# A projection of un-normed activations: moving the RMS factor behind the expert query product

## What is computed

```python
h = x + mixed                                   # mixed: output projection of the attention block
return h + peer_ffn(rmsnorm(h, norm2_gain), peer_w_q, peer_sub_keys, peer_u, peer_v)

def _rms(x):
    return xf * lax.rsqrt(jnp.mean(xf * xf, axis=-1, keepdims=True) + EPS)
def rmsnorm(x, gain):
    return _rms(x) * gain

def peer_ffn(x, w_q, sub_keys, expert_u, expert_v):
    q = _rms((xt @ w_q).reshape(T, P_HEADS, P_KEY_DIM))     # 8 heads of 256
    s1 = einsum('thd,hnd->thn', q[..., :half], sub_keys[:, 0])
    s2 = einsum('thd,hnd->thn', q[..., half:], sub_keys[:, 1])
    ...                                         # top 16 of each half, then of their sums, softmax
    a = einsum('cd,ckd->ck', xc, expert_u[ec])  # the normed x again
    return einsum('ck,ckd->cd', g * gelu(a), expert_v[ec])
```

## Time and profile before

| | |
|---|---|
| median of 3 runs | 2245.87 us |
| lowest and highest run | 2237.79 and 2246.01 us |
| span of the profiled execution | 2240.8 us |
| PE busy in it | 2181.3 us, 97% |
| DVE busy | 1581.9 us, 71% |
| ACT busy | 1063.3 us, 47% |
| POOL busy | 501.9 us, 22% |

### The profile page before, as it was taken

The page is one execution under the profiler, slowest core; times in us unless marked ns, Lnnn a source line. Parts: engine busy times, 40 slices in busy tenths (PEclk is TensorE's granted clock), DMA queues, the critical chain, the costliest instruction groups (busy, mean ns, idle before and its releaser), DMA issues.

```text
span 2240.8 us, 35063 instructions
## 1 busy us (share of the span) xinstructions
PE 2181.3 (97%) x12495; PEld 1938.3 (87%) x12495; DVE 1581.9 (71%) x3249; ACT 1063.3 (47%) x1934; POOL 501.9 (22%) x387
## 2 busy tenths in 40 slices
PE   6999999999999988899999999999999999999999
PEld 4888888888878446668899999999999999999999
DVE  5444444433366687452488899999988899999996
ACT  5444344323243477633444445888864333333332
POOL 0000000000030000010000123655435555555550
PEclk9999999999999999999999999999999999999999
DMA  5222222222234100023355888999999999999993
GB/s 177 90 94 93 84 84 85 93 94 94 94 129 160 57 1 1 1 63 116 109 178 163 256 259 303 371 401 386 397 340 404 414 399 389 397 395 389 396 401 139
DMA packets 134241, 475.74 MB, mean 212 GB/s; under 512 B 14448, under 2 KB 30832, under 8 KB 132192
## 3 DMA queue, kind: packets, MB, share of 16 engines
q1 hardware_dynamic: 74592, 232.29, 30.1%
q0 software_dynamic: 55920, 212.36, 24.8%
q10 hardware_dynamic: 3600, 29.36, 3.2%
HBM read 422.58 MB, written 50.86 MB: 211 GB/s over the span
## 4 chain that ended last, share of the span: by engine, by line
PE 90%; DVE 7%; ACT 2%; issue 1%; DMA 0%; ACTq 0%; DVEq 0%
PE bank L469 18%; PE bank L471 17%; PE bank L470 17%; PE bank L1190 8%; PE bank L1192 8%; PE bank L1191 8%; PE bank L1162 4%; PE bank L484 2%; PE bank L584 1%; DVE wlo L456 1%; PE bank L544 1%; DVE rows L2207 1%; PE bank L778 1%; PE bank L796 1%; ACT pair_prob L1416 1%; PE bank L761 1%
## 5 line engine op out<-in xcount | busy, mean ns | idle before, releaser
L469 PE MATMUL bank<-act_hi,whi 128*128 128x352 f32 (+1 forms) x1968 | 713.9, 363 | 9.9 <-DVE act_lo L1688 5.8
L470 PE MATMUL bank<-act_lo,whi 128*128 128x352 f32 (+1 forms) x1968 | 702.6, 357 | 0.0
L471 PE MATMUL bank<-act_hi,wlo 128*128 128x352 f32 (+1 forms) x1968 | 702.4, 357 | 0.0
L456 DVE TENSOR_TENSOR wlo<-raw,whi 128x1024 fp32r<-128x1024 f32 x398 | 485.2, 1225 | 269.3 <-ACT whi L452 267.3
L452 ACT ACTIVATE whi<-raw 128x1024 fp32r<-128x1024 f32 x398 | 418.7, 1057 | 394.5 <-PE bank L1192 330.9
L469 PEld LDWEIGHTS bank<-act_hi,whi 128*128 128x128 f32 x1968 | 370.5, 188 | 59.2 <-issue 18.2
L471 PEld LDWEIGHTS bank<-act_hi,wlo 128*128 128x128 f32 x1968 | 370.2, 188 | 37.7
L470 PEld LDWEIGHTS bank<-act_lo,whi 128*128 128x128 f32 x1968 | 370.7, 188 | 35.9 <-issue 0.5
L1190 PE MATMUL bank<-h_hi,whi 128*128 128x384 f32 x1024 | 342.5, 334 | 1.8 <-issue 1.8
L1191 PE MATMUL bank<-h_lo,whi 128*128 128x384 f32 x1024 | 342.5, 334 | 0.0
L1192 PE MATMUL bank<-h_hi,wlo 128*128 128x384 f32 x1024 | 342.5, 334 | 0.0
(11 more groups left out here) (377 smaller groups left out, 2522.0 us busy)
## 6 DMA issues: line engine op xcount, KB each, us to landing
raw<-tiles SPq DMA_DIRECT2D x398, 512.0 KB, 4.9
gates_dram<-stage ACTq DMA_DIRECT2D x12, 2048.0 KB, 11.8
wg<-gates_dram POOLq DMA_DIRECT2D x16, 1536.0 KB, 13.3
acts_dram<-gelu SPq DMA_DIRECT2D x120, 192.0 KB, 5.7
hf<-acts_dram POOLq DMA_DIRECT2D x30, 768.0 KB, 10.4
bias<-alibi POOLq DMA_DIRECT2D x16, 256.0 KB, 2.9
w1s<-cmp_w POOLq DMA_DIRECT2D x1, 4096.0 KB, 13.3
res<-x_t ACTq DMA_DIRECT2D x4, 512.0 KB, 6.1
```

Source lines behind the costliest of these rows:

```text
L456: dve.tensor_tensor(wlo[:, j.slot, :], raw[:, j.slot, :], whi[:, j.slot, :].bitcast(F32), ALU.subtract).then_inc(lo_made, 1)
L469: pe.matmul(to, wh, x, start=(kc == 0), stop=False)
L470: pe.matmul(to, wh, xl, start=False, stop=False)
L471: last = pe.matmul(to, wl, x, start=False, stop=(kc == KC - 1))
```

## The change

The query projection takes `res * gain` instead of the normed input.

- As each J_E result is added to the residual, ACT also writes `raw_hi` = res * gain rounded, and DVE `raw_lo`, the rest (`make_raw_lo`). All 16 jobs of J_F multiply these. The two first jobs are no longer interleaved.
- POOL adds up the squares of all eight chunks (chunks 1 to 7 onto chunk 0, now in `sqe`), and PE sums them with one `add_squares` between jobs 0 and 1 of J_F. Four narrow matmuls beside it put the same sums in token order in bank 7, from which DVE makes EPS * (mean + EPS) as `eps_col`.
- The root, the Newton step and the normed input `xnrm` (two buffers, one chunk for each job) are made beside jobs 0 to 8 of J_F; `turn_x` stands inside jobs 2 to 9. J_U waits for all eight low parts.
- The head norm's `ms` adds `eps_col` in place of EPS.
- `raw_lo` lies where `subk` goes, so POOL loads `subk` when job 15 of J_F is done, in place of job 1.

```diff
@@ pool
-            for c in range(1, 6):
-                add_up(sq, 3 * KC + c + 1, c)
+            for c in range(1, KC):
+                add_up(sqe, 3 * KC + c + 1, c)
 
-            pool.wait_ge(job_done, J_F + 1 + RING)
+            pool.wait_ge(job_done, J_F + 16 + RING)
             pool.dma_start(subk[:, :, :], sub_keys).then_inc(S("subk_landed"), 16)
@@ tensor
-            for m, chunk in enumerate((0, 6, 7)):
-                pe.wait_ge(*((S("sq_added"), 15) if m == 0 else (sq_made, 3 * KC + chunk + 1)))
-                last = add_squares(4, sq[:, chunk, :], m == 0, m == 2)
-            last.then_inc(sums_made, 1)
+            def width_sums():
+
+                pe.wait_ge(S("sq_added"), 10 + KC - 1)
+                for tt in range(TT):
+                    pe.matmul(bank[7][:, 2 * tt:2 * tt + 2], sqe[:, 0, tt * P:(tt + 1) * P], ones[:, 0:2],
+                              start=True, stop=True)
+                add_squares(4, sqe[:, 0, :], True, True).then_inc(sums_made, 1)
...
-            two_jobs(Job(J_F), Job(J_F + 1), 3 * KC, turn_x)
+            multiply(pe, Job(J_F), raw_hi, raw_lo, chunk_normed(3 * KC))
+            width_sums()
+            multiply(pe, Job(J_F + 1), raw_hi, raw_lo)
             for m in range(2, 16):
-                multiply(pe, Job(J_F + m), act_hi, act_lo)
+                beside = (lambda kc: turn_x(m - 2) if kc == 4 else None) if m - 2 < KC else None
+                multiply(pe, Job(J_F + m), raw_hi, raw_lo, beside)
+            pe.wait_ge(lo_act, 5 * KC)
@@ scalar
-                square(sq[:, m, :], res[:, m, :], sq_made)
-            root(6, 0, 4, D)
-            for c in range(8):
-                act.wait_ge(normed, 3 * KC + c + 1)
-                copy(act_hi[:, c, :], hg[:, c, :], hi_act)
+                square(sqe[:, m, :], res[:, m, :], sq_made)
+                copy(raw_hi[:, m, :], res[:, m, :], hi_act, g("norm2", m))
             for m in range(16):
                 j = Job(J_F + m)
                 make_hi(act, j.ahead())
+                if m == 0:
+                    root(6, 0, 4, D, xnrm[:, 0, :])
                 result_of(act, j)
...
+                if m < KC:
+                    act.wait_ge(normed, 3 * KC + m + 1)
+                    copy(act_hi[:, m, :], xnrm[:, m % 2, :], hi_act)
@@ vector
+            def make_raw_lo(kc):
+                dve.wait_ge(hi_act, 3 * KC + kc + 1)
+                dve.scalar_tensor_tensor(out=raw_lo[:, kc, :], in0=res[:, kc, :], scalar=g("norm2", kc),
+                                         in1=raw_hi[:, kc, :].bitcast(F32), op0=ALU.mult, op1=ALU.subtract)\
+                    .then_inc(lo_act, 1)
...
+                if m:
+                    make_raw_lo(m - 1)
+            make_raw_lo(7)
...
-            invert(6, 0)
-            split_activations(lambda kc: (res[:, kc, :], hg[:, kc, :]), "norm2", 0, 3 * KC)
             for m in range(16):
                 make_lo(dve, Job(J_F + m).ahead())
+                if m == 0:
+                    invert(6, 0, xnrm[:, 0, :], xnrm[:, 1, :])
+                    dve.tensor_scalar(eps_col, ..., EPS / D, EPS * EPS, ALU.mult, ALU.add)
+                if m < KC:
+                    if m >= 2:
+                        dve.wait_ge(S("x_step"), m - 1)
+                        dve.wait_ge(lo_act, 4 * KC + m - 1)
+                    dve.scalar_tensor_tensor(out=xnrm[:, m % 2, :], in0=res[:, m, :], scalar=g("norm2", m),
+                                             in1=rrow[:, 0, :], op0=ALU.mult, op1=ALU.mult).then_inc(normed, 1)
+                if 1 <= m <= KC:
+                    make_act_lo(xnrm[:, (m - 1) % 2, :], 4 * KC, m - 1)
```

More of the change, by code:

```diff
@@ L363, in two_layer_kernel @@
         subk = at("subk", R + 16 * KB, [P, 16, P])
+        raw_hi = at("raw_hi", R, [P, KC, T], F32R)
+        raw_lo = at("raw_lo", R + 16 * KB, [P, KC, T], F32R)
+        sqe = at("sqe", R + 64 * KB, [P, KC, T])
+        xnrm = at("xnrm", R + 96 * KB, [P, 2, T])
+        eps_col = mx[:, 0:TT]
         ssb = at("ssb", R, [P, 16, P])
@@ L697, in _ @@
             pool.dma_start(wukv[:, :, :, :], w_ukv).then_inc(S("w_mla_landed"), 16)
-            for c in range(1, 6):
-                add_up(sq, 3 * KC + c + 1, c)
-            pool.wait_ge(job_done, J_F + 1 + RING)
+            for c in range(1, KC):
+                add_up(sqe, 3 * KC + c + 1, c)
+            pool.wait_ge(job_done, J_F + 16 + RING)
             pool.dma_start(subk[:, :, :], sub_keys).then_inc(S("subk_landed"), 16)
-            power(2, 32)
+            power(3, 32)
             def load_gates(grp):
@@ L1100, in turn_x @@
                 cols_ = slice((kc % 4) * P, (kc % 4 + 1) * P)
-                turn(pe, bank[5 + kc // 4][:, cols_], hg[:, kc, 0:P], ident)
+                turn(pe, bank[5 + kc // 4][:, cols_], xnrm[:, kc % 2, 0:P], ident)
                 for s in range(4):
-                    x = pe.matmul(bank[(4, 7)[kc // 4]][32 * s:32 * s + EXTRA, cols_], hg[:, kc, P:FIRST], ident,
+                    x = pe.matmul(bank[(4, 7)[kc // 4]][32 * s:32 * s + EXTRA, cols_], xnrm[:, kc % 2, P:FIRST], ident,
                                   start=True, stop=True)
-                if kc == KC - 1:
-                    x.then_inc(S("x_step"), 1)
-            two_jobs(Job(J_F), Job(J_F + 1), 3 * KC, turn_x)
+                x.then_inc(S("x_step"), 1)
+            multiply(pe, Job(J_F), raw_hi, raw_lo, chunk_normed(3 * KC))
+            width_sums()
+            multiply(pe, Job(J_F + 1), raw_hi, raw_lo)
             for m in range(2, 16):
-                multiply(pe, Job(J_F + m), act_hi, act_lo)
+                beside = (lambda kc: turn_x(m - 2) if kc == 4 else None) if m - 2 < KC else None
+                multiply(pe, Job(J_F + m), raw_hi, raw_lo, beside)
+            pe.wait_ge(lo_act, 5 * KC)
             def u_job(n):
@@ L1115, in _ @@
             pe.wait_ge(S("halves_added"), 8)
-            pe.wait_ge(S("x_step"), 5)
+            pe.wait_ge(S("x_step"), KC + 4)
             for h in (0, 1, 2, 3, 4, 5, 6, 7):
@@ L1120, in _ @@
             u_job(1)
-            pe.wait_ge(S("x_step"), 7)
+            pe.wait_ge(S("x_step"), KC + 6)
             for b in range(2):
@@ L1135, in _ @@
             pe.wait_ge(S("subk_landed"), 16)
-            pe.wait_ge(ms_made, 2)
+            pe.wait_ge(ms_made, 3)
             routes(0)
@@ L1214, in _, with root @@
             make_hi(act, Job(0))
-            def root(n, slot, b, width):
+            def root(n, slot, b, width, mean=mean):
                 act.wait_ge(sums_made, n)
@@ L1529, in _ @@
                 act.sem_inc(acts_stored[slot], 16)
-            act.wait_ge(S("x_step"), 1)
+            act.wait_ge(S("x_step"), KC)
             for h in range(2):
@@ L2170, in _ @@
             dve.wait_ge(ssq_made, 4)
+            dve.wait_ge(ms_made, 1)
             for b in range(2):
                 sums = bank[(4, 7)[b]][:, :].rearrange("p (t j r) -> p t j r", t=TT, j=4)[:, :, :, 0:1]
-                dve.tensor_scalar(ms[:, 0:32].rearrange("p (t b j) -> p t b j", t=TT, b=2)[:, :, b, :],
-                                  sums.rearrange("p t j r -> p t (j r)"), 1.0 / 256, EPS, ALU.mult, ALU.add)\
+                dve.scalar_tensor_tensor(out=ms[:, 0:32].rearrange("p (t b j) -> p t b j", t=TT, b=2)[:, :, b, :],
+                                         in0=sums.rearrange("p t j r -> p t (j r)"), scalar=1.0 / 256,
+                                         in1=eps_col.unsqueeze(2).broadcast_to((P, TT, 4)), op0=ALU.mult, op1=ALU.add)\
                     .then_inc(ms_made, 1)
@@ L2213, in use_row @@
                                              op0=ALU.mult, op1=ALU.add).then_inc(S("row_used"), 1)
-            dve.wait_ge(S("x_step"), 5)
+            dve.wait_ge(S("x_step"), KC + 4)
             for tt in range(TT):
```

5 lines of the change are left out of this document (4 added, 1 removed).

## The result

The changed kernel takes 2220.85 us, the median of 12 runs (2217.93 to 2229.2). The kernel before, run between them on the same chip, takes 2237.06 us (12 runs, 2228.26 to 2247.23). The ratio is 0.9942, interval 0.9924 to 0.996.

The account below looks back on a forecast made before the run. PE, busy 97% of the span, was taken as the bound. Jobs 87.04, turns 5.56 and sums 1.73 us make 94.33 instead of 101.62, a gain of 7.3; 2245.87 - 7.3 = 2238.6 us, range 2229 to 2246.

Parts of the forecast that it names:

- The sum: PE from J_E's end to J_U's start: 101.62 us before, 94.33 us after, a gain of 7.3 us.
- sixteen jobs and eight `turn_x`: PE's work in J_F: 16 jobs at 5.44 us make 87.04 us, eight turns at 0.695 make 5.56 us.
- square sums: PE in J_F: one remaining sum 0.86 us plus four narrow matmuls 0.87, together 1.73 us, bounds 1.1 to 1.75.
- the narrow matmuls: Four two-column matmuls on PE, taken to count as eight 128 x 128 transposes: 0.87 us, lower bound 0.2.
- The clock: PE from J_E's end to J_U's start: granted clock 1.00 throughout, as 0.50 stood only behind PE's 3.7 us wait.
- The inputs: Start of J_F: PE never pauses; slack 1.7 us for chunk 7, 2.0 for POOL's sum; rival of a partial pause 12%.
- the rule of the Trainium skill: Two-input DVE and POOL SBUF instructions lock each other out; chunk 7's low part would come at 992.4, slack 0.5 us.
- my budget of 2.68 of 2.72 us: Jobs 0 to 3 of J_E: DVE's work of 0.69 + 1.23 + 0.76 us just fits the 2.72 us between jobs.
- `subk`: Load issued about 76 us later, landing after 5.1 us, cover 9 us before first `routes`; rival of late landing 3%.
- The gain reaches the end: Behind J_F all work hangs on PE, so a rigid shift: the 7.3 us also come off the span, to 2233.5 us.
- The level of the time: Whole kernel: 7.3 us off the median 2245.87 gives 2238.6 us, with spans and times spreading over some 8 us.
- Faster by over 0.5%: Whole kernel: faster by more than about 11 us needs a low draw of the runs on top of the gain; 15%.

Follow-up runs that it names:

- the second profile: The changed kernel run again without an edit: 2230.31 us, ratio 0.998 to the kernel before.
- `subk_late`: On the kernel before, only the `subk` load moved, to wait for job 15 of J_F in place of job 1: 2228.61 us, ratio 0.9994.
- `after`: First measurement and profile of the changed kernel, against the kernel before: 2220.85 us, ratio 0.9942; profiled span 2227.5 us.

## Why the prediction was wrong, point by point

**The sum: right.** Forecast 94.33 us from J_E's end to J_U's start; measured 94.38, and 94.39 in the second profile. Term by term: sixteen jobs and eight `turn_x` together 92.63 by the trace (94.38 less 1.75 of sums) against 92.60; square sums 1.75 against 1.73, the narrow matmuls 0.80 against 0.87. That they count as eight instructions was the upper bound that I took. In exchange the sum on PE took 0.95 us, forecast 0.86. The gain of this stretch is 7.24 us, forecast 7.3.

**The clock: right, and for the reason named.** 1.00 throughout. Both runs that bring a pause back show the granted clock below it again. I had seen it after a wait of 3.7 us; the runs show it after 2.8 as well.

**The inputs: no pause, as forecast, but a reading of the rows was wrong.** I took the 1.23 us of a weight split beside a 1.81 us addition on POOL as no slowing, and weighed against it the rule of the Trainium skill ("SBUF — State Buffer", section "SBUF: two separate sides"), which these rows seemed to refute. I had looked at DVE's row alone. In this pair DVE came first and POOL waited: its 1.81 was already lengthened, 1.29 being its time alone. Five of the eight `raw_lo` then took 1.78 us. By my budget of 2.68 of 2.72 us for a J_E job, DVE had no room for another microsecond in jobs 0 to 3, and it ran late there: the residual additions at 969.36 and 972.80 are 3.44 us apart instead of 2.72. PE did not wait, because DVE has time again in the last jobs (1.36, 1.37 and 4.09 us of idle ahead of the last three additions). Chunk 7's low part was ready at 992.41 and job 0's chunk 7 starts at 993.69, so 1.3 us were left; by the rows I had 1.7, by the rule 0.5. That 992.41 looks like the 992.4 worked out by the rule is chance, for J_E ended 0.78 us later here. Counted from J_E's end, the low part was ready after 3.5 us, where the rule gave 4.25 and the rows 3.05. The rule's sum was too long because it took 1.81 us for POOL's last addition, which took 1.30: POOL ended 2.9 us behind J_E, not 3.45. The high part took 0.71 us (at most 0.7).

**`subk`: right.** It was issued 70.4 us later (forecast about 76) and landed after 5.1 us, with no wait; moving it alone changes no level.

**The gain reaches the end: right.** From J_U's start to the end of the span the kernel before takes 1144.2 us in `subk_late`'s trace and the changed kernel 1144.2 in `after`'s, both with the same distances in J_U. (The four traces of the changed kernel have 1144.2 three times and 1145.8 once, so some 1.6 us can vary there by itself.) The shift is rigid; DVE's and DMA's busy stages gave nothing back. The lowest levels differ by 7.76 us, the middle ones by 6.99.

**The level of the time: wrong.** This is the step that failed. I wrote that "spans and times of this kernel spread over some 8 us", took that for a scatter around the median of three, and laid the gain on that median: 2245.87 - 7.3 = 2238.6. The kernel before has levels at 2227.8, 2236.8 and 2245.5, and three runs had shown one of the middle and two of the highest. On the mean of 112 runs the same sum gives 2234.7 - 7.3 = 2227.4, and the mean of 48 runs of the changed kernel is 2226.75. The range's lower end, 2229, was the lowest of three runs less the largest gain; the true lowest level less the gain forecast is 2220.5, measured 2220.06. The trace that I had held a sign: 352-column matmuls at 166.7 ns from 1108 and at 158.3 from 1251 with the clock at 1.00 in both. I had not compared a matmul's distance across stages, only checked that PE was busy.

**Faster by over 0.5%.** The first comparison gave 0.58%, the three others of the changed kernel 0.2, 0.29 and 0.42%, the levels 0.31 to 0.35%. The 15% that I gave to it was for a "low draw of the runs on top of the gain", and that is what the first comparison was: 2220.85 is the lowest level, 2237.06 the middle one of before.

## What to carry to other kernels

Compare a stage between two profiles by the distance from start to start of one kind of matmul, not only by busy time and clock: it shows at once what of a difference belongs to the edit (here 7.2 us of 13.3). Where single runs stand on levels, compare level with level and count how many are on each; a median of 12 can move by a whole level, 9 us here, with nothing changed. And a chain of small steps on other engines (sum, root, first chunk) that PE waits for costs its own length and then the half clock behind it, so take it out from in front of PE whole: putting back just the 2.8 us wait for the additions cost 4.6 us.

## What was not expected of the hardware

- A 352-column matmul in 32-bit precision with rounded operands follows its like after 158.3 or 166.7 ns at a granted clock of 1.00, one of them for a hundred microseconds and more, changed at pauses as short as 0.29 us, or behind a single distance of 208 ns. 158.3 is the mean of an uneven row of four, 155 to 161. 336 columns show 153.3 and 155.8; 320, 368, 384 and 512 one each: 146.7, 166.7, 173.3, 226.7.
- DVE's `raw_lo` (two large operands in SBUF) takes 0.75 us alone and 1.78 beside an addition on POOL, the addition 1.29 alone and 1.81 beside DVE's weight split. In these rows the first to start keeps its time.
- A pause of 2.8 us on PE was followed by 1.2 GHz: 0.69 granted over the next 5.45 us. The clock did not fall in the pause itself: the granted clock was still 1.00 for 1.85 us of work behind it, then 0.51 for 3.3 us.
